# An encoder layer's opening: norm weight by transposes, other banks and order for the first token tiles, bias lines on four row groups

## What is computed

```python
u = rms_norm(h, g_norm)                    # x * rsqrt(mean(x*x) + eps) * g_norm
z = einsum('bsd,dc->bsc', u, w_in)         # q, k, v, gates and the LRU input from one projection
bias = rel_bias[t5_bucket(kpos - qpos)]    # per head, depends on kpos - qpos only
s = einsum(q, k) + bias                    # differential attention, two softmaxes
w = softmax(s[0]) - lam * softmax(s[1])    # lam = exp(lam_q1.lam_k1) - exp(lam_q2.lam_k2) + lam_init
log_a = -8 * r * softplus(-lru_lambda)     # decay of the linear recurrence on channels
y = conv_b + sum(xp[t] * conv_w[t])        # width-4 convolution, ahead of the LRU's gates
h = h + mix @ w_out; h = h + rms_norm((p @ w_ple) * sigmoid(h @ w_pg), g_ple)
```

## Time and profile before

| | kernel before |
|---|---|
| median of 3 runs | 1090.42 us |
| the profiled execution | 1091.32 us, its span 1089.5 us |
| PE busy | 1040.7 us, 96% of the span |
| DVE, ACT, POOL busy | 651.1, 571.8, 497.5 us |
| chain of work that ended last | PE 60%, DVE 21%, issue 9%, ACT 4%, POOL 3% |
| granted TensorE clock, mean | 0.995 |

### The profile page before, as it was taken

One profiled execution on the slowest core, in us unless ns is written; L12 is line 12 of the kernel. 1 busy time (PEld: TensorE's weight loads), 2 busy tenths in 40 slices (PEclk: granted clock), 3 DMA queues, 4 the chain that ended last, 5 costly groups with the idle time before them and its releaser, 6 DMA issues.

```text
span 1089.5 us, 15394 instructions
## 1 busy us (share of the span) xinstructions
PE 1040.7 (96%) x5776; PEld 823.3 (76%) x5776; DVE 651.1 (60%) x1047; ACT 571.8 (52%) x859; POOL 497.5 (46%) x397
## 2 busy tenths in 40 slices
PE   4999999999999999998999999999998999999997
PEld 3777777777777888875777777777776888888786
DVE  5651635537258324049999999999964255455423
ACT  6415557484463213149999999999852122112112
POOL 5312334341557553006676776766566143434421
PEclk9999999999999999999999999999998999999999
DMA  8134362321325633939965567363293232342220
GB/s 278 63 95 135 107 220 79 135 98 57 117 70 163 197 116 88 287 98 229 239 172 153 157 173 210 94 166 118 67 296 136 63 117 83 111 135 83 83 97 39
DMA packets 115529, 147.70 MB, mean 136 GB/s; under 512 B 10200, under 2 KB 79448, under 8 KB 115416
## 3 DMA queue, kind: packets, MB, share of 16 engines
q1 hardware_dynamic: 115456, 146.73, 44.9%
HBM read 99.44 MB, written 47.25 MB: 135 GB/s over the span
## 4 chain that ended last, share of the span: by engine, by line
PE 60%; DVE 21%; issue 9%; ACT 4%; POOL 3%; DMA 2%; SPq 1%; DVEq 0%; POOLq 0%; ACTq 0%
DVE E_ L1478 10%; PE b_ps L1654 6%; PE b_ps L1656 6%; PE b_ps L1655 6%; PE b_ps L1740 5%; PE b_ps L1738 5%; PE b_ps L1739 5%; PE uT_ps L1694 4%; PE g_ps L1654 3%; PE g_ps L1656 3%; PE g_ps L1655 3%; PE o_ps L1798 2%; PE w_ps L1781 2%; PE s_ps L1751 2%; DVE ratio L1487 2%
## 5 line engine op out<-in xcount | busy, mean ns | idle before, releaser
L1123 ACT ACTIVATE E_<-E_,nmax 128x1024 f32<-128x1024 f32 (+1 forms) x184 | 186.7, 1018 | 15.0 <-DVE nmax L1478 14.7
L1478 DVE CUSTOM_DVE_ANT_0 E_<-s_ps,bias 128x1024 f32<-128x1024 f32 (+1 forms) x184 | 188.0, 1056 | 3.6 <-PE s_ps L1751 3.6
L877 POOL TENSOR_TENSOR E_<-E_,ratio 128x576 f32<-128x576 f32 (+3 forms) x92 | 84.6, 919 | 85.7 <-DVE E_ L1494 85.7
L1654 PE MATMUL b_ps<-u_hi,wA_hi 128*128 128x512 f32 x288 | 119.8, 416 | 3.1 <-DVE u_lo L1285 3.1
L1656 PE MATMUL b_ps<-u_hi,wA_lo 128*128 128x512 f32 x288 | 113.1, 393 | 0.0
L1655 PE MATMUL b_ps<-u_lo,wA_hi 128*128 128x512 f32 x288 | 112.8, 392 | 0.0
L880 POOL TENSOR_TENSOR E_<-E_ 128x576 f32<-128x576 f32 (+3 forms) x92 | 103.7, 1127 | 7.2
L1751 PE MATMUL s_ps<-KL,QL 128*128 128x512 f32 x256 | 90.3, 434 | 14.0 <-DVE nmax L1478 13.3
L1781 PE MATMUL w_ps<-ident,E_ 128*128 128x128 f32 x624 | 83.5, 273 | 1.8 <-ACT WT L1151 1.7
L1151 ACT ACTIVATE WT<-w_ps 128x1024 f32<-128x1024 f32 (+1 forms) x96 | 83.3, 868 | 2.8 <-PE w_ps L1781 2.6
L1798 PE MATMUL o_ps<-WT,V 128*64 128x128 f32 x1280 | 84.0, 278 | 0.0
(11 more groups left out here) (206 smaller groups left out, 2265.5 us busy)
## 6 DMA issues: line engine op xcount, KB each, us to landing
z_ch<-z_stage SPq DMA_DIRECT2D x36, 256.0 KB, 2.2
QL<-qk_t SPq DMA_DIRECT2D x32, 256.0 KB, 6.3
KL<-qk_t SPq DMA_DIRECT2D x32, 256.0 KB, 7.6
bias<-line_d SPq DMA_DIRECT2D x8, 960.0 KB, 11.3
x_sb<-in_x SPq DMA_DIRECT2D x12, 512.0 KB, 4.6
wA_raw<-in_w_in SPq DMA_DIRECT2D x12, 512.0 KB, 4.1
qk_t<-qh SPq DMA_DIRECT2D x24, 256.0 KB, 2.3
qk_t<-ql SPq DMA_DIRECT2D x24, 256.0 KB, 2.8
```

Source lines behind the costliest of these rows:

```text
L1123: act.activation(e, e, ACT.Exp, bias=nmax[:, n % 5, c:c + 1], scale=-1.0, accum_out=sums[:, n % 5, c:c + 1]).then_inc(e_done, 1)
L1478: dve.tensor_tensor_reduce(weights_at(n)[:, c, 0:n_tok], s_ps[:, c, 0:n_tok], b[:, ::-1], -1.0, 3e38, ALU.add, ALU.min, nmax[:, n % 5, c:c ...
L1654: pe.matmul(dst, sh, mh, start=k == 0, stop=False)
```

## The change

The norm weight is loaded as a 4 KB tile g_col (channel by partition, eight columns) from ACT's queue; PE spreads it by eight transposes of broadcast columns into PSUM, and DVE copies that to gnB. The 512 KB broadcast load is gone. The first token tiles use other banks (tile 2 those of b_ps); DVE's order becomes normalise 0, 1, 2, u_low 0, normalise 3, u_low 1, u_low 2, and from n = 3 on u_low(n) and then normalise(n+1). ACT squares four tiles first. POOL's wA_low(0) and (1) move forward by one tile. In block 0 the transposes stand at k = 3 and k = 6. The one-hot table is laid out on four groups of 32 partitions, rel_bias is loaded four times, and the four line products stand together behind block 4, each on its own row group and bank. Their copies on ACT stand together, still ahead of the two Exp. store_z(2) to (4) move ahead of the wait for the lines, and the wait for line_out moves from DVE (before lru_clear) to ACT's decays(0, 0).

```diff
--- before.py
+++ after.py
@@ -144,8 +144,9 @@
         lam_sb = sb("lam_sb", [P, 4, HQ], F32, ph1a)
         lam_w = sb("lam_w", [P, 3, 2 * HQ], F32, ph1a)
         sp_w = sb("sp_w", [P, 4, 2 * LC], F32, ph1a)
-        rb_sb = sb("rb_sb", [NBUCKET, HEADS], F32, ph1a)
-        oh_sb = sb("oh_sb", [NBUCKET, LINE], F32, ph1a)
+        g_col = sb("g_col", [P, KC], F32, ph1a)
+        rb_sb = sb("rb_sb", [P, HEADS], F32, ph1a)
+        oh_sb = sb("oh_sb", [P, 512], F32, ph1a)
         line_st = sb("line_st", [HEADS, LINE], F32, ph1a)
         ph1a.close()
 
@@ -293,7 +294,7 @@
         pp3.close()
 
 
-        const_in = sem("const_in"); gnB_in = sem("gnB_in"); oh_in = sem("oh_in")
+        const_in = sem("const_in"); gnB_in = sem("gnB_in"); gn_turned = sem("gn_turned")
         ident_done = sem("ident_done"); chain = sem("chain")
         line_ps = sem("line_ps"); line_sb = sem("line_sb"); line_out = sem("line_out")
         lam_exp = sem("lam_exp"); lam_dot = sem("lam_dot");
@@ -380,7 +381,9 @@
             return o_ps[:, 1, :] if j < IN_STEPS or j % 2 else g_ps[:, 1, :]
 
         def uT_slot(n):
-            return (uT_ps[:, 0:2, :].rearrange("p a b -> p (a b)") if n % 2 == 0 else
+            if n == 2:
+                return b_ps[:, 1:3, :].rearrange("p a b -> p (a b)")
+            return (uT_ps[:, 0:2, :].rearrange("p a b -> p (a b)") if n == 0 or n % 2 and n > 1 else
                     qT_ps[:].rearrange("p a b c -> p (a b c)"))
 
         ZB = [(0, 0), (1, 0), (0, 1), (1, 1), (0, 2), (2, 0), (1, 2), (2, 1), (2, 2)]
@@ -416,7 +419,7 @@
 
         def line_bank(b):
 
-            return uT_ps[0:HEADS, 2, :]
+            return uT_ps[0:HEADS, b, :] if b < NB else qT_ps[0:HEADS, 0, :, :].rearrange("p a b -> p (a b)")
 
         UNITS = {0: (SHORT, 0), 1: (LONG, SHORT)}
         TOK0 = SHORT
@@ -446,18 +449,18 @@
                              ).then_inc(wA_in[m % 3], 16)
 
             load_x(0)
-            sp.dma_start(gnB[:], bass.AP(tensor=g_norm.tensor, offset=0, ap=[[0, P], [1, D]])).then_inc(gnB_in, 16)
             load_x(1)
             load_x(2)
             load_x(3)
             load_wA(0)
             load_x(4)
-            sp.dma_start(rb_sb[:], rel_bias).then_inc(oh_in, 16)
-            sp.dma_start(oh_sb[:], onehot).then_inc(oh_in, 16)
             load_x(5)
             load_wA(1)
             load_x(6)
             load_x(7)
+            sp.dma_start(oh_sb[:], onehot).then_inc(const_in, 16)
+            for b in range(4):
+                sp.dma_start(rb_sb[NBUCKET * b:NBUCKET * b + NBUCKET, :], rel_bias).then_inc(const_in, 16)
             sp.dma_start(chan_sb[:], chan).then_inc(const_in, 16)
             sp.dma_start(norm_sb[:], norms).then_inc(const_in, 16)
             sp.dma_start(lam_sb[:], bass.AP(tensor=lams.tensor, offset=0, ap=[[0, P], [HQ, 4], [1, HQ]])
@@ -517,10 +520,10 @@
 
             store_z(0)
             store_z(1)
+            for i in range(2, 5):
+                store_z(i)
             sp.wait_ge(line_sb, 4)
             sp.dma_start(line_d, line_st[:]).then_inc(line_out, 16)
-            for i in range(2, 5):
-                store_z(i)
             load_wA(3)
             sp.wait_ge(lru_clear, 1)
             load_lru(0)
@@ -837,9 +840,9 @@
 
             for n in range(NT):
                 x_scale(n)
-                if n == 4:
+                if n == 3:
                     wA_low(0)
-                if n == 6:
+                if n == 5:
                     wA_low(1)
                 if n == 11:
                     wA_low(2)
@@ -954,6 +957,7 @@
 
         @block.scalar
         def _(act):
+            act.dma_start(g_col[:], g_norm).then_inc(gnB_in, 16)
             act.sem_inc(v_evac, 2)
 
             def square_x(n):
@@ -1007,6 +1011,8 @@
                 act.wait_ge(sig_done, 2 * u + 2)
                 if u:
                     act.wait_ge(scan_done, u)
+                else:
+                    act.wait_ge(line_out, 16)
                 act.activation(A_[:], R_[:], ACT.Exp, scale=nrate[:, c, e:e + 1]).then_inc(a_done, 1)
                 if c and e == 0:
                     act.wait_ge(sum_done, c)
@@ -1025,21 +1031,20 @@
                     act.activation(wB_hi[g][:, 2 * j:2 * j + 2, :], wB_raw[g][:, 2 * j:2 * j + 2, :], ACT.Copy
                                    ).then_inc(wBhi_done, 1)
 
-            for n in range(3):
+            for n in range(4):
                 square_x(n)
             for n in range(NT):
                 split_u(n)
-                if n + 3 < NT:
-                    square_x(n + 3)
+                if 2 <= n < NT - 2:
+                    square_x(n + 2)
                 if n == 1:
                     wA_high(0)
                 if n == 3:
                     wA_high(1)
                 if n == 8:
                     wA_high(2)
-                if n in (6, 8, 10):
-                    line_up((n - 6) // 2)
-            line_up(3)
+            for b in range(4):
+                line_up(b)
             act.wait_ge(lam_dot, 1)
             act.activation(lam_w[:, 2, 0:2], lam_w[:, 1, 0:2], ACT.Exp).then_inc(lam_exp, 1)
             act.wait_ge(lam_dot, 2)
@@ -1271,7 +1276,10 @@
                 ins.then_inc(chain, 1)
                 dve.wait_ge(chain, links[0])
 
-            dve.wait_ge(gnB_in, 16)
+            dve.wait_ge(gn_turned, 1)
+            dve.tensor_copy(gnB[:], uT_slot(1)).then_inc(chain, 1)
+            links[0] += 1
+            dve.wait_ge(chain, links[0])
 
             def normalise(n):
                 dve.wait_ge(x_rs, n + 1)
@@ -1297,16 +1305,21 @@
                     dve.tensor_tensor(z_stage[:, i % NB, :], z_stage[:, i % NB, :], b_ps[:, i % NB, :], ALU.mult
                                       ).then_inc(z_evac, 1)
 
-            normalise(0)
-            for n in range(NT):
+            for n in range(3):
+                normalise(n)
+            u_low(0)
+            normalise(3)
+            u_low(1)
+            u_low(2)
+            for n in range(3, NT):
+                u_low(n)
                 if n + 1 < NT:
                     normalise(n + 1)
-                u_low(n)
                 if n in (5, 7, 9):
                     z_out_of_psum((n - 5) // 2)
 
 
-            dve.wait_ge(const_in, 48)
+            dve.wait_ge(const_in, 128)
             dve.tensor_scalar(gains[:, 0:1], norm_sb[:, 0:1], ATTN_SCALE, None, ALU.mult)
             dve.tensor_copy(gains[:, 1:2], norm_sb[:, 1:2])
             dve.tensor_scalar(gains[:, 2:3], norm_sb[:, 2:3], 1.0 - LAM_INIT, None, ALU.mult)
@@ -1341,7 +1354,6 @@
             z_out_of_psum(3)
             dve.wait_ge(uT_done, NT)
             dve.wait_ge(x_sq, NT)
-            dve.wait_ge(line_out, 16)
             for a, b in ((0, 2), (2 + LONG, 5 + LONG), (XPAD - 1, XPAD)):
                 dve.memset(XP[:, a:b], 0.0)
             dve.memset(R_[:, GAP0:GAP1], 0.0)
@@ -1658,18 +1670,18 @@
 
             def transpose_u(n):
                 pe.wait_ge(u_done, n + 1)
-                if n >= 2:
-                    pe.wait_ge(ulo_done, n - 1)
+                if n >= 3:
+                    pe.wait_ge(ulo_done, n - 1 if n > 4 else n - 2)
                 for k in range(KC):
                     mm = pe.transpose(uT_slot(n)[:, k * P:(k + 1) * P], u_tok[:, n % 2, k * P:(k + 1) * P], ident[:])
                 mm.then_inc(uT_done, 1)
 
-            def line(b):
-                pe.wait_ge(oh_in, 32)
-                if b:
-                    pe.wait_ge(line_sb, b)
-                pe.matmul(line_bank(b), rb_sb[:], oh_sb[:, b * 512:(b + 1) * 512], start=True, stop=True
-                          ).then_inc(line_ps, 1)
+            def lines():
+                pe.wait_ge(const_in, 128)
+                for b in range(4):
+                    rows = slice(NBUCKET * b, NBUCKET * b + NBUCKET)
+                    pe.matmul(line_bank(b), rb_sb[rows, :], oh_sb[rows, :], start=True, stop=True
+                              ).then_inc(line_ps, 1)
 
             def z_block(i, between=None):
                 m, b = ZB[i]
@@ -1695,18 +1707,23 @@
                                    start=True, stop=True)
                 mm.then_inc(gate_mm, 1)
 
+            pe.wait_ge(gnB_in, 16)
+            for k in range(KC):
+                mm = pe.transpose(uT_slot(1)[:, k * P:(k + 1) * P], g_col[:, k:k + 1].to_broadcast([P, P]), ident[:])
+            mm.then_inc(gn_turned, 1)
             for n in range(4):
                 transpose_u(n)
             for i in range(4):
                 def more_tokens(k):
-                    if k == 1:
+                    if k == (1 if i else 3):
                         transpose_u(4 + 2 * i)
-                    if k == 5:
+                    if k == (5 if i else 6):
                         transpose_u(5 + 2 * i)
 
                 z_block(i, more_tokens)
-                line(i)
-            for i in range(4, 8):
+            z_block(4)
+            lines()
+            for i in range(5, 8):
                 z_block(i)
```

(4 more changed lines are left out.)

## The result

The changed kernel takes 1099.44 us (median of four runs, 1098.01 to 1103.11) against 1090.62 us; the ratio is 1.009, with a 95% interval of 1.0076 to 1.0104. A later comparison gave 1102.22 against 1090.0, ratio 1.0109 (1.0091 to 1.0126). The profiled execution is the longest of the first four, 1103.11 us with a span of 1101.3, against 1091.32 and 1089.5. It was forecast at 1102.8 (1091.32 + 11.5), and the median at 1101.9.

The account below looks back on a forecast made before the run. PE's program order was taken to bound the first 90 us, shifts passing through one to one. A gate 9.3 us late plus 2.2 for the clock made 11.5 on 1090.42: 1101.9 us, range 1095 to 1105.

Parts of the forecast that it names:

- The opening: First token tiles, up to the input projection's first matmul: block 0 starts at 19.0, 3.1 us earlier.
- The upper end: Latest time given for normalise(0) in the opening: 9.2, were the small load as slow as the large one.
- The clock in the opening: Transposes and start of block 0: PE stays at the low level, transpose 4 at 22.9.
- rival (b): Opening: the clock rises during back-to-back transposes, block 0 starts at the high level; 2.7 us less, 1099.2; 15%.
- The closed round: Tiles 4 to 11: 4.6 us between transposes against PE's 3.7, PE idles 0.9 a tile; block 4 0.8 late.
- The queue behind the lines: Block 4 to first gate: line copies delay the Exp, sp_w chain and load_wA(3); gate at 90.0, 9.3 us late.
- The clock at the gate: First gate: 5.0 us of PE idle time lowers the clock, + 2.2 us (bounds 0 and 3).
- The sum: Whole kernel: 9.3 + 2.2 = 11.5 us added to the median of 1090.42, giving 1101.9.
- Rival (a): First gate: the clock stays up over the 5 us idle time, 1099.7; 15%.
- Rival (e): Opening to gate: PE's own work alone sets the pace, 3.1 and about 3.4 us are won, 1083.9; 5%.

Follow-up runs that it names:

- the token order alone: Changed kernel with normalise(n+1) ahead of u_low(n) again on DVE from tile 4 on: 1093.14 us, ratio 1.0028.

## Why the prediction was right

**The opening** came 0.5 us sooner than worked out (18.48 against 19.0). The small load took 2.4 us and not 3.2, and normalise(0) stood at 6.82 in place of 7.4, at the lower end given, where rsx is there: its row names POOL's rsx as what it waited for, and in the other profiles of this kernel's relatives, where the load took 1.6 to 1.8 us, the first set starts no earlier than 8.13. The upper end, 9.2, is 9.5 by its own terms (0.8 + 5.3 + 1.97 + 1.2 + 0.2); nothing hung on it. PE turned three tiles without a gap; the fourth waited 0.43 us for its tile, and tile 3's split then stood behind a square in ACT's queue (16.07, the transposes having ended at 15.6), which used up what the faster fourth set had won. How the 3.66 us of the earlier start divide among the load, the banks and DVE's order is not shown, but for 0.56 us that u_low(3) ahead of normalise(4) gave by itself (21.58 against 22.14).

**The clock in the opening** was the place where the forecast chose wrongly between two cases: it kept the low level up to block 0, and rival (b) had the high level there. Both happened in turn. The level rose during the back-to-back transposes, as 14.50 shows with 1.09 us, and fell again in the 2.89 us idle time before block 0. The outcome for the time was that of the forecast, since block 0 began low; that was luck in part, as in the execution with the token order alone it began high. The sentence of the Trainium skill (TensorE: Matmul & The Clock Gate, Part 4: PE-mode transpose) that transposes do not count as PE-busy in the same way is not borne out here: where page and measurement differ, the measurement decides.

**The closed round** was worked out at 4.6 us and measured at 4.66; PE idles 0.82 us a round (0.9 forecast) and 1.48 where nine matmuls lie between (1.6). The 0.06 us more, six times from transpose 5 to 11, and 0.08 at block 4 ate most of the 0.5 us of the better start: block 4 at 59.36, forecast 59.45. That this order is the cause is shown from both sides: turned back it gave 7.3 us (52.03 for block 4, with the Exp moved too), put into the kernel before, its four stalls took 3.8.

**The queue behind the lines** went as followed through, each step within 0.15 us: Exp 68.07 (68.2), DVE 68.29 (68.4), z_out_of_psum(3) 73.23 (73.3), load 75.43 (75.5), convolution 83.30 (83.2), gate 90.05 (90.0). The durations of the earlier trace rows carried over unchanged, because nothing else moved relative to this chain.

**The clock at the gate** was right in kind and small in size: 2.2 us forecast, 2.8 to 3.0 measured from gate to gate. The term was taken from 4.7 us at the low level; here it held for 5.7 us of work, a gate's six matmuls and the first of block 8 (90.05 to 95.73). And one step was off: PE was to be idle for 5.0 us before the gate; it was 3.21, as block 6, behind 2.38 us of idle time, ran at the low level from 75.3 to 78.7. The forecast had looked only at an idle time of 4.44 us and had no term for this one. It cost nothing at the gate. Nor does it come each time: both profiles of the changed kernel have this low stretch, the kernel whose only edit is the matmuls ahead of block 0 has none behind an idle time of 2.37 us, and there PE idles 4.64 us before the gate, close to the 5.0.

**The sum** for the profiled execution was 1102.8, measured 1103.1: the clock took 0.6 us more than its term, and the rest of the kernel 0.3 less than before. The median of the first runs lies 2.5 us under the forecast, that of the repeat 0.3 above it. The shorter runs have the mean clock of 0.991 to 0.994 in place of 0.988, as if one or two low stretches were missing; which ones can't be read, as those runs have no trace. Rival (a), the clock stays up, stood at 1099.7. Two kernels in which extra matmuls hold it up measured 1099.22, with the gate 1.35 us early through the opening, and 1101.49, with the gate 0.5 us late through the fill; an estimate corrected for both, from one profile each, is 1100.6 and 1101.0, so the price was about 1 us low. The clock at the gate, with an early rise in the opening, may be what the shorter runs show. That stays open without a profile of one.

**Rival (e)**, PE alone sets the pace, stood at 1083.9. The kernel with both orders turned back measured 1084.38: the price was right, and what kept the change from it were two orders of instructions.

## What to carry to other kernels

When work is moved in one engine's queue, ask what stands behind it there: four copies moved behind a later product cost 7 us through two 0.2 us operations queued after them. A producer that is put behind the consumer of its own output closes a loop. Add up the loop's round and compare it with the work the bound engine has for each round, including work that the same change takes away. And where PE's idle time can't be removed, matmuls whose result nobody reads can hold the clock up; they pay if they end before the wait does (0.5 us was lost where they did not).

## What the runs showed of the hardware

- The granted level rose while PE did nothing but transposes back to back (three sets of 1.9 to 1.97 us, the fourth 1.09), and it fell in the following 2.9 us without work. The fourth set takes 1.09 or 1.10 us in all ten profiles with this opening. In the kernel before, with gaps of 0.5 to 1.3 us between the sets, all four take 1.94 to 1.97.
- Behind an idle time of 2.38 us that followed rounds with 0.8 us of idle time each, the level fell again in both profiles of the changed kernel, though PE was at work when it did (75.3 us in the first); in the two with the fill it did not, and neither in the kernel whose only extra matmuls stand ahead of block 0, which leaves that idle time empty. So what decides it there is not shown.
- Behind the idle time before the gate (3.0 to 4.6 us) the level was low in all five profiles that have it, and in none of the two with the fill, at 8.06 and 8.15 us from gate to gate in place of 9.67 to 11.16.
- Four products of 32 rows on four row groups took 0.97 us in place of 3.66, 3.8 times. The last 0.3 us of the 3.66 were at the low level, six of the eight records taking 2.58, so at the high level the ratio would be slightly less. The Trainium skill (TensorE: Matmul & The Clock Gate, Part 3: Packing small matmuls) has 3.07 for such a packing; here the measured number stands.
- Behind the 3.66 us of products with 32 rows and 8 columns on one group, block 5 began at the low level (0.80 us for its first matmul in place of 0.50), though PE had not been idle. That the few rows and columns in use are the reason was not tried, and it is one execution.
